# First block's modulations: partial sums over rows on VectorE beside the mixers' input products

## The reference, cut to what matters

```
cond = silu(c)
for l in range(2):                                   # first block
    mod = cond @ w_ada[l] + b_ada[l]                 # 1024 x 6144 weights per layer
    shift1, scale1, gate1, shift2, scale2, gate2 = split(mod, 6)
    h = x * (1 + scale1) + shift1
    x = layer_norm(ALPHA * x + gate1 * token_mixer(h), ...)
    h = x * (1 + scale2) + shift2
    x = layer_norm(ALPHA * x + gate2 * moe_ffn(h), ...)
```

## Time and profile before

| | |
|---|---|
| median of three runs | 3406.43 us |
| the profiled execution's own time | 3408.06 us |
| its span | 3406.3 us |
| mean granted clock of TensorE | 0.961 |
| PE busy | 3082.4 us (90%) |
| DVE busy | 1133.4 us (33%) |
| ACT busy | 614.5 us (18%) |
| DMA | 702.73 MB, mean 206 GB/s |

### The profile page before, as it was taken

The page is one execution under the profiler, slowest core; times in us unless marked ns, Lnnn a source line. Parts: engine busy times, 40 slices in busy tenths (PEclk is TensorE's granted clock), DMA queues, the critical chain, the costliest instruction groups (busy, mean ns, idle before and its releaser), DMA issues.

```text
span 3406.3 us, 70549 instructions
## 1 busy us (share of the span) xinstructions
PE 3082.4 (90%) x30752; PEld 2285.9 (67%) x30752; DVE 1133.4 (33%) x2231; ACT 614.5 (18%) x1174; POOL 216.3 (6%) x188
## 2 busy tenths in 40 slices
PE   7989998888989998887999999999988798887999
PEld 5767555556768565555856544588878777786888
DVE  1245332223245332223545221003244453445100
ACT  0111111111111111112323110000223222331100
POOL 0000000000000000000000000000034302430000
PEclk9999999999999999998999999999999999998999
DMA  7565999997565999997135212244310032000442
GB/s 284 185 247 235 420 421 418 420 420 273 183 251 221 420 420 417 420 420 307 50 136 203 107 62 74 99 148 148 130 62 4 4 109 100 4 4 10 165 149 99
DMA packets 99617, 702.73 MB, mean 206 GB/s; under 512 B 11328, under 2 KB 11504, under 8 KB 16608
## 3 DMA queue, kind: packets, MB, share of 16 engines
q1 hardware_dynamic: 95584, 685.47, 51.1%
q0 software_dynamic: 3712, 12.61, 1.1%
HBM read 696.98 MB, written 1.05 MB: 205 GB/s over the span
## 4 chain that ended last, share of the span: by engine, by line
PE 76%; DMA 12%; DVE 7%; ACT 2%; issue 2%; SPq 1%; POOL 0%; DVEq 0%; ACTq 0%; POOLq 0%
PE ps L229 18%; PE ps L1659 10%; PE ps L1646 9%; PE ps L1181 8%; PE ps L2291 7%; DMA arena<-in_w_up 7%; PE ps L1998 4%; DMA arena<-in_w_down 4%; PE ps L1209 3%; DVE arena L162 2%; PE ps L373 2%; PE ps L577 2%; PE ps L1267 2%; PE ps L604 2%; ACT arena L145 1%
## 5 line engine op out<-in xcount | busy, mean ns | idle before, releaser
L229 PE MATMUL ps<-arena 128*128 128x256 f32 (+1 forms) x2208 | 527.7, 401 | 18.9 <-ACT arena L145 11.2
L145 ACT ACTIVATE arena<-ps 128x512 f32<-128x512 f32 (+1 forms) x486 | 250.9, 516 | 1495.8 <-PE ps L1646 292.9
L229 PEld LDWEIGHTS ps<-arena 128*128 128x128 f32 x2208 | 427.1, 195 | 117.4 <-issue 47.1
L1181 PE MATMUL ps<-arena 128*32 128x256 f32 (+2 forms) x5120 | 409.5, 407 | 56.3 <-DMA arena<-in_w_up 54.8
L1181 PEld LDWEIGHTS ps<-arena 128*32 128x32 f32 (+2 forms) x5120 | 257.0, 125 | 212.3 <-issue 124.4
L2291 PE MATMUL ps<-arena 64*64 64x64 f32 x10496 | 306.4, 225 | 61.2 <-issue 23.4
L2291 PEld LDWEIGHTS ps<-arena 64*64 64x64 f32 x10496 | 293.2, 140 | 75.0 <-issue 38.7
L1646 PE MATMUL ps<-arena 128*128 128x512 f32 (+1 forms) x1024 | 332.3, 486 | 3.5 <-DVE arena L171 3.4
L1659 PE MATMUL ps<-arena 128*128 128x256 f32 x1536 | 332.0, 379 | 0.0
L162 DVE TENSOR_TENSOR arena<-arena,ps 128x512 f32<-128x512 f32 (+1 forms) x264 | 158.1, 599 | 517.6 <-PE ps L2291 244.9
L1659 PEld LDWEIGHTS ps<-arena 128*128 128x128 f32 x1536 | 291.8, 190 | 40.1 <-issue 0.5
(11 more groups left out here) (210 smaller groups left out, 2445.6 us busy)
## 6 DMA issues: line engine op xcount, KB each, us to landing
arena<-in_w_gate SPq DMA_DIRECT2D x128, 1024.0 KB, 18.2
arena<-in_w_up SPq DMA_DIRECT2D x128, 1024.0 KB, 19.6
arena<-in_w_down SPq DMA_DIRECT2D x128, 1024.0 KB, 18.9
arena<-in_mlp SPq DMA_DIRECT2D x80, 1024.0 KB, 4.8
arena<-in_w_ada SPq DMA_DIRECT2D x48, 1024.0 KB, 7.3
arena<-in_ada SPq DMA_DIRECT2D x48, 1024.0 KB, 5.1
arena<-in_w_in SPq DMA_DIRECT2D x30, 1024.0 KB, 6.4
arena<-in_w_rkv SPq DMA_DIRECT2D x20, 1024.0 KB, 4.8
```

The costliest lines, as they stand in the source:

```text
L145: self.e.activation(out, in_, func, bias=bias, scale=scale, **more).then_inc(*self.done(key))
L229: ins = pe.matmul(out, a, b, start=start and i == 0, stop=stop and i == len(pairs) - 1)
L1181: ins = pe.matmul(psum.of["gu", l, new][o:o_, i_ * 256:i_ * 256 + 256], xe[:, k, new % 2 * 128 + o:new % 2 * 128 + o_], w[i_].rearrange("p ...
```

## The change

The first block's 48 pieces leave the pumps; PIECES now has only the second block's 48. The host lays the first block's weights out by input rows: a piece n now holds, for each of the 128 partitions, two of its eight rows of 1024 columns. DVE multiplies each row by its number of the condition and adds them up over the eight rows of the partition (two operations of 128x1024 per piece, four pieces a vector), into one of two buffers `partial`. PE then sums over partitions only: for the gates two products of a matrix of ones with 512 columns each, for the other vectors eight products with one column of ones, each with another 128x128 part of the sums as stationary. DVE adds the bias.

The pieces of vectors 0 and 1 (layer 0) are loaded and summed ahead of mixer 0. Those of vectors 2 to 7 are loaded, two behind each w_in group, in mixer 0 (groups 0 to 11), those of vectors 8 to 11 in mixer 1 (groups 0 to 7). PE's sums stand in the middle of groups 2, 4, 6, 8 and so on; DVE's part of groups 3 to 6 stands before the rotation, that of group 7 behind the statistics, that of 8 to 12 behind the norm of Z. The ring has NRING + NAHEAD = 8 slots from the mixer's start to its last pump; the two `partial` buffers lie where slot 8 of the experts' ring is, which therefore waits for the last sum. Pumps behind w_in groups and in the experts go; those in the attentions and features stay.

```diff
-NPUMP = (2, 6)
+NAHEAD = 3
+        def partial_dve(dve, do, n):
+            u, q, a, w = n // 4, n % 4, partial[n // 4 % 2], weights.of["mod piece", n]
+            dve.wait_ge(*at["mod piece", n])
+            if q == 0 and u > 1:
+                dve.wait_ge(*at["mod sums", u - 2])
+            for k in (2 * q, 2 * q + 1):
+                src = w[:, k % 2 * 1024:k % 2 * 1024 + 1024]
+                if k == 0:
+                    do.ts(a, src, cond[:, 0:1], None, ALU.mult, None)
+                else:
+                    do.stt(a, src, cond[:, k:k + 1], a, ALU.mult, ALU.add, ("summed", n) if k % 2 else None)
+        def sums_of_partial_pe(pe, u):
+            l, v = VECTORS[u]
+            a = partial[u % 2]
+            reach(pe, *at["summed", 4 * u + 3])
+            if v in (2, 5):
+                for h in range(2):
...
+                    ins = pe.matmul(b[:, :], ones[:, :], a[:, h * 512:h * 512 + 512], start=True, stop=True)
+            else:
...
+                for k in range(8):
+                    ins = pe.matmul(b[:, k:k + 1], a[:, k * 128:k * 128 + 128], ones[:, 0:1], start=True, stop=True)
+            ins.then_inc(*made(("mod sums", u)))
         def mixer_sp(sp, pump, l):
-            pump.until(0, l, 0, 1)
+            weights.size = NRING + NAHEAD
+            if l == 0:
+                for n in range(4 * FROM[0]):
+                    partial_sp(sp, n)
             for i in range(15):
                 load(sp, ("w_in", l, i), ("pz" if i < 7 else "gates", l, i, 1), D["w_in"][l, i])
-                if i >= 9:
-                    pump()
+                for n in pieces_at(l, i):
+                    partial_sp(sp, n)
             for h in range(16):
                 pump()
+            weights.size = NRING
+            weights.used[NRING + NAHEAD] = [("mod sums", FROM[l + 1] - 1)]
...
         def mixer_pe(pe, pump, l):
-            pump.until(0, l, 0, 1)
             turned_pe(pe, l, 0, lambda t: ("ln", ("moe", l - 1), t) if l else "x")
+            if l == 0:
...
+                for n in range(4 * FROM[0]):
+                    reach(pe, *at["mod piece", n])
+                    keep_warm(pe, b, 4)
+                for u in range(FROM[0]):
+                    sums_of_partial_pe(pe, u)
...
+                    if t == 0:
+                        for u in vector_at(l, i):
+                            sums_of_partial_pe(pe, u)
...
-                if i >= 9:
-                    pump()
+                    if c == 0:
+                        for u in vector_at(l, i):
+                            sums_of_partial_pe(pe, u)
         def mixer_dve(dve, pump, l):
...
             for i in range(3):
+                modulations(i)
...
+            modulations(3, 4, 5, 6)
             dve.wait_ge(*at["mixer", l])
             rope_dve(dve, do, ("mixer", l), M.q4, M.t4, 2, 10, M.g3, M.tb[:, 0], M.tb[:, 1], pairs)
...
-            pump()
+            modulations(7)
             dve.wait_ge(*at["sgu root", l])
...
-            for _ in range(3):
-                pump()
+            modulations(8, 9, 10, 11, 12)
         def moe_sp(sp, l):
-                for _ in range(n):
-                    pump()
-                if p == NR - 2:
-                    pump.until(0, l, 5)
```

More of the change, by code:

```diff
@@ L261, in program @@
         small = sb("small", 512)
-        ones32 = sb("ones32", 128)
         routing = sb("routing", 832)
@@ new lines, in mods_dve @@
+        def mods_dve(dve, do, u):
+            l, v = VECTORS[u]
+            dve.wait_ge(*at["mod sums", u])
+            if v in (2, 5):
+                dve.wait_ge(*at["gate bias", l, v])
+                for h in range(2):
+                    dst = gate[v // 3][:, h * 512:h * 512 + 512]
+                    do.tt(dst, psum.of["mod sums", u, h][:, :], dst, ALU.add, ("mod added", u, h))
+            else:
+                o = l * 32 + {0: 0, 1: 1, 3: 2, 4: 3}[v] * 8
+                do.stt(mod1[:, o:o + 8], psum.of["mod sums", u, 0][:, 0:8], 1.0 if v in (1, 4) else 0.0,
+                       vecs[:, VO[f"b_ada{l}"] + o - l * 32:VO[f"b_ada{l}"] + o - l * 32 + 8], ALU.add, ALU.add,
+                       ("mod added", u, 0))
+            if at.counting:
+                at.known["mod", 0, l, v, 3] = formed.now()
@@ L336, in program @@
+        PIECES = [(1, l, v, q) for l in range(2) for v in range(6) for q in range(4)]
         class Pump:
             def __init__(self, opens, closes=None):
-                self.opens, self.closes, self.open, self.next, self.limit = opens, closes, None, 0, 56
+                self.opens, self.closes, self.open, self.next = opens, closes, None, 0
             def __call__(self):
@@ L360, in opens @@
             def opens(n, blk, l, v, q):
-                load(sp, ("ada", n), ("ada rows", n), D["w_ada" if blk == 0 else "ada2"][l, v * 4 + q])
+                load(sp, ("ada", n), ("ada rows", n), D["ada2"][l, v * 4 + q])
             return Pump(opens)
@@ L380, in closes @@
                 reach(pe, *at["ada stage", n])
[L381 to L386, removed]
+                reach(pe, *at["ident"])
+                for c in range(2):
+                    ins = pe.transpose(b[:, c * 128:c * 128 + 128], st[:, c * 128:c * 128 + 128], ident[:, :])
                 ins.then_inc(*made(("ada turned", n)))
@@ L401, in closes @@
                 dve.wait_ge(*at["ada turned", n])
[L402 to L421, removed]
-                    do.stt(mod2[:, o:o + 4].rearrange("p (c s) -> p c s", c=2), tmp, 0.0, bc(vecs[:, bo:bo + 2], 2, 2),
-                           ALU.add, ALU.add)
-                    at_mod = formed.now()
+                view = b[:, 0:256].rearrange("p (c j s r) -> p c s j r", c=2, j=4, s=2)[:, :, :, :, 0]
+                tmp = small[:, 0:4].rearrange("p (c s) -> p c s", c=2)
+                o = l * 96 + v * 16 + 4 * q
+                bo = VO[f"b2_{l}"] + v * 8 + 2 * q
+                do.red(tmp, view, ALU.add, ("ada out", n))
+                do.stt(mod2[:, o:o + 4].rearrange("p (c s) -> p c s", c=2), tmp, 0.0, bc(vecs[:, bo:bo + 2], 2, 2),
+                       ALU.add, ALU.add)
+                at_mod = formed.now()
                 if at.counting:
@@ L1313, in moe_act @@
                 gather(0, k)
-            for p, new, Q, ks, n in rounds(l):
+            for p, new, Q, ks in rounds(l):
                 if p >= 0:
```

81 lines of the change are left out of this document (47 added, 34 removed).

## The result

| | before | after |
|---|---|---|
| median of the first comparison, us | 3406.43 (3397.44 to 3413.26, 5 runs) | 3375.86 (3364.97 to 3388.69, 5 runs) |
| profiled execution: own time, span | 3408.06, 3406.3 | 3364.97, 3363.2 |
| mean clock, profiled execution | 0.961 | 0.960 |
| mean clock, all executions of the study | 0.956 to 0.965 | 0.948 to 0.960 |

The ratio is 0.9912, 95% interval [0.9897, 0.9928]; the forecast was 3366.1. Profile against profile the gain is 43.1 us (forecast 40.4), at the medians only 30.6, and a later comparison (label a_same) gave 3389.47 against 3405.61, ratio 0.9959 [0.9945, 0.9974]. The forecast lies 9.8 us under the first median and 23.4 under the second. The profiled execution of after was the fastest of its five. So there are two questions: whether the steps came out as worked out, and where the rest goes in the other executions.

The account below looks back on a forecast made before the run. PE was taken to bound input products and second-block attention, DMA the expert stretches. Terms -20.0-20.6-5.0-2.6+5.9+1.9 = -40.4 us from the profiled 3408.1, less 1.6 to the median, gave 3366.1 us, range 3351 to 3390.

Parts of the forecast that it names:

- the expert streams: Both layers' expert stretches: 8 loads of 1.049 MB leave, 5.0 us in the first and 15.0 in the second, -20.0 us.
- the start: Before mixer 0's input products: PE starts them at 45.5 us, -2.6 us, ends -5 and +3.
- the wait of PE in the middle of step 8: Each mixer's w_in products: PE's sum waits for DVE's pieces of step 7, 8.3 us in each mixer.
- the input products: Mixers' w_in products get slower: +5.9 us in mixer 0, +1.9 in mixer 1; together ends -6 and +22.
- The features: Second block's last features: three pump passes go, -5 us, ends -1.5 and -5.5.
- Rival C: Input products: DVE becomes the bound as its operations slow beside landing loads; turns at about 4.2 us a piece; 3437 us, chance 0.05.
- the lower clock behind the wait: Mixers' input products: PE runs at the lower clock after its wait for DVE, another 3.0 us.
- A sum over partitions: PE's sum of one vector, 8 products of 2 instructions: 2.0 us, ends 1.4 to 3.5.
- rival A: Second block's heads: DVE and ACT take over at some 3.2 us a head, -10.5 instead of -20.6, 3377 us; chance 0.12.
- heads 16 to 31: Second block's attention: 16 pumps of 1.37 us go, some 0.65 us of wait at two borders, -20.6 us, ends -21.9 and -10.

Follow-up runs that it names:

- a_same: The changed kernel once more, nothing edited; 3389.47 us against 3405.61 us before, ratio 0.9959.
- c: The changed kernel with 2 extra unused loads of 1.049 MB in layer 0's experts and 6 in layer 1's; 3395.95 us.
- f: The changed kernel with one more DVE operation of 128x1024 per piece (4.0 us a piece instead of 2.65); 3408.21 us, ratio to before 0.9993.
- b: The changed kernel with PE's sums of vectors 5, 6, 7 and 11 placed later in the mixers; 3350.59 us, ratio to before 0.9856.
- g: The changed kernel with the second block's 16 attention pumps in heads 16 to 31 instead of 0 to 15; 3406.38 us, ratio to before 0.9982.
- i: The changed kernel with later sums, vector 0 summed early, and 2 idle PE products per head in heads 17 to 31; 3358.08 us.

## Why the prediction was right, and where it was off

*Right in mechanism and size:* the expert streams (c shows that loads alone make the price in layer 1), the start, the wait of PE in the middle of step 8 (8.54 and 8.55 us against 8.3), its place, and that the input products get slower while the gain lies elsewhere. The features are right in the first profile (-5.3 against -5) and some -3.5 in most others. Rival C's turning point was put at 4.2 us a piece; f at 4.0 is at zero, but that agreement is in part luck, since its zero holds the clock of the heads, which C's sum hadn't. C's reason, an operation that gets slower beside landing loads, isn't there (1.28 us).

*Mis-sized:* the lower clock behind the wait. The step took 3.0 us from the stall of before; measured are 1.9, since the clock had fallen while PE stood and rose at the end of the gate sum. The windows of the wait, of the sum and of the step behind it:

```profile
111.54:120.09 8.55, 0.01 (x1) 0.00 (x0) 7.98 (x10) 2.73 (x5) 0.00 (x0) 0.63 0.48 178
120.09:123.67 3.58, 3.58 (x5) 1.51 (x6) 3.39 (x5) 0.00 (x0) 0.00 (x0) 0.50 1.01 403
123.67:130.70 7.03, 7.03 (x33) 6.21 (x32) 6.45 (x8) 0.38 (x1) 0.00 (x0) 0.98 0.35 120
```

A sum over partitions was taken as 2.0 us, from 64 columns; in the stream it takes 1.70 (95.79 to 97.49), 0.106 an instruction.

*Luck:* the 40.4 against 43.1 of the profiles. The heads gave 4.3 us less than the sum had, and 5.8 us came from stretches that the sum had at nothing, by their clock; the profiled execution was also the one with the highest clock of its five. The median of 3375.86 lies beside rival A's 3377, but not for A's reason alone: A's 3.2 us a head didn't come (2.48), and the larger part is clock.

*Wrong:* heads 16 to 31, at -20.6. "A head takes ... 1.37 us: 16 heads" is right for a single head (2.48 from 1827.96 to 1830.44), but a group of eight takes 23.06 us (1820.32 to 1843.38), where the forecast makes it 21.7 (32.02 before, from 1841.45 to 1873.47, less 8 x 1.37, plus 0.65): DVE and ACT come late at some value products and at the group's end (1.21 us instead of 0.65). The first and the last four heads have such waits too, 1.04 us for DVE at 1818.43 and 1.42 for ACT at 1855.43. Rival A had this at a larger size. In all it is 4.3 us. The greater miss is that the step knew of no clock: in executions like a_same it is worth 3.8 us. The sentence "with only scores and turning left ahead of it" saw the thinner work and drew only the wait from it. The profiled execution hid this, the medians show it: 12.5 us in the narrow heads, 9.1 in the wide ones and 5.8 in the mixer make 27.3 between the two profiles of one kernel (21.9 in all, since other stretches give 5.4 back).

The wide heads and the mixer's attention keep their pumps and yet lose the clock in some executions of after (clock of before: never under 0.956). What decides how long the first fall in the wide heads lasts (3.5 to 20.5 us with the same pumps), and so why b kept the clock mostly and a_same in none of six, stays open. That the length of this fall and the fate of the unfilled narrow heads go together is read from seven profiles; no run separates them.

## What to carry to other kernels

Here the work that filled a bound engine's stretch also held its clock: before moving such work out, ask what the clock does in the thinner stretch, look at several executions' mean clock beside their times, and don't trust one profile. Side work belongs where it costs least per piece and each stretch keeps some of it: two pieces in one short stage cost 2.04 us for the second, one each in two stages 1.0 to 1.4. A late partial sum costs the wait at its consumer, so put the consumer where the producer's line ends, not where the loop index is even.

## What was not expected of the hardware

- TensorE stayed at 1.2 GHz for 112.6 us at a busy share of 98.8% (g), and two idle products of 256 columns per head, 0.97 us in a head of mostly 3.4, went with 2.4 GHz for the whole stretch (i: clock 1.00, one profile).
- DVE's first product of a vector, a tensor-scalar operation over 128x1024 in fp32, takes 0.75 us and the multiply-add over the same elements 1.28 (84 of them, 107.9 us). The Trainium skill's page "VectorE: DVE Perf Modes", section "What auto-detection actually checks", says that an operation gets a double rate if its single source and its destination are in SBUF, with even or equal outer dimensions. By that rule the first product has the double rate and the multiply-add, with two sources, hasn't; the trace agrees in the order and shows a factor of 1.7 for the whole instruction.
- Weights landing at 398 GB/s beside DVE's reads of the same ring changed nothing in DVE's time: 1.28 us, as in the earlier trace rows. A load of a piece took 11.2 us to land, 7.3 before.
